# Gate and state stores of an mLSTM/GLA decoder step issued by SP behind the weight loads, in place of ScalarE

## What is computed

```python
a = rmsnorm(h, g_mix)
z = a @ w_in                      # 1024 x 8216: q, k, v and gates of both branches
hm, C, n, m = mlstm_scan(mq, mk, mv, li, lf, C0, n0, m0)
hg, Sf = gla_scan(gq, gk, gv, la, S0)
hm = head_layernorm(hm) * g_m * sigmoid(mo)
hg = head_rmsnorm(hg) * g_g * silu(gg)
h = h + (sigmoid(ga) * (hm @ w_pa) + sigmoid(gb) * (hg @ w_pb)) @ w_o
h = h + conv_ffn(rmsnorm(h), ...)           # w_up, depthwise conv, w_down
h = h + sigmoid(rmsnorm(h) @ w_ple_gate) * (p @ w_ple_proj)
y = rmsnorm(h, g_out)
```

## Time and profile before

| | |
|---|---|
| median of 3 runs | 1183.09 us |
| the profiled execution | 1183.06 us |
| its span, first to last instruction | 1181.2 us |
| TensorE busy | 1166.8 us (99%) |
| VectorE busy | 757.9 us (64%) |
| ScalarE busy | 393.1 us (33%) |
| first and last moved store issued | 115.3 us and 533.4 us |
| DMA on the SP queue, on ScalarE's queue | 89.39 MB, 47.77 MB |

### The profile page before, as it was taken

How to read it: one execution, slowest core, us unless ns; L and a number is a source line. 1 busy time by engine, 2 the same in 40 slices (tenths; PEclk the granted TensorE clock), 3 DMA queues, 4 the chain that set the end, 5 groups by cost and what they waited for, 6 DMA issues and landing times.

```text
span 1181.2 us, 21812 instructions
## 1 busy us (share of the span) xinstructions
PE 1166.8 (99%) x9169; PEld 1110.0 (94%) x9169; DVE 757.9 (64%) x1396; ACT 393.1 (33%) x576; POOL 2.3 (0%) x7
## 2 busy tenths in 40 slices
PE   9999999999999999999999999999999999999996
PEld 8999999999999999999999999999999999999995
DVE  6855568675777655664655667777777763333777
ACT  6243232134343322333343233333333322111544
POOL 0000000000000000000000000000000000000000
PEclk9999999999999999999999999999999999999998
DMA  6342232422312366563443542232222143223222
GB/s 220 112 145 90 90 108 90 144 72 93 113 67 109 133 228 212 177 199 120 153 155 114 172 147 72 72 108 72 75 105 72 61 163 107 72 94 98 77 99 81
DMA packets 48962, 138.56 MB, mean 117 GB/s; under 512 B 5460, under 2 KB 25108, under 8 KB 39776
## 3 DMA queue, kind: packets, MB, share of 16 engines
q1 hardware_dynamic: 16392, 89.39, 21.9%
q10 hardware_dynamic: 32472, 47.77, 12.0%
HBM read 113.15 MB, written 23.81 MB: 116 GB/s over the span
## 4 chain that ended last, share of the span: by engine, by line
PE 95%; issue 3%; DVE 1%; DMA 1%; ACT 1%; POOL 0%; ACTq 0%; POOLq 0%; DVEq 0%
PE ps L768 34%; PE ps L796 10%; PE ps L794 6%; PE ps L797 6%; PE ps L795 6%; PE ps L897 6%; PE ps L774 6%; PE ps L798 5%; PE ps L903 3%; PE ps L815 2%; PE aux L1060 1%; DMA xT<-in_xT 1%; PE aux L1124 1%; PE aux L955 1%; PE aux L1020 1%
## 5 line engine op out<-in xcount | busy, mean ns | idle before, releaser
L768 PE MATMUL ps<-apair,whi 128*128 128x288 f32 x1728 | 274.9, 298 | 0.6 <-ACT mq L2067 0.5
L768 PEld LDWEIGHTS ps<-apair,whi 128*128 128x128 f32 x1728 | 243.2, 188 | 4.9 <-issue 2.1
L1175 DVE TENSOR_TENSOR wlo<-wraw,whi 128x2048 fp32r<-128x2048 f32 (+1 forms) x82 | 176.1, 2147 | 74.8 <-ACT whi L1912 70.5
L1912 ACT ACTIVATE whi<-wraw 128x2048 fp32r<-128x2048 f32 (+1 forms) x87 | 156.4, 1797 | 106.2 <-PE ps L798 52.5
L796 PE MATMUL ps<-apair,whi 128*128 128x512 f32 x336 | 132.1, 393 | 0.0
L794 PE MATMUL ps<-apair,whi 128*128 128x320 f32 x336 | 105.0, 313 | 0.0
L797 PE MATMUL ps<-apair,wlo 128*128 128x320 f32 x336 | 104.2, 310 | 0.0
L795 PE MATMUL ps<-apair,whi 128*128 128x320 f32 x336 | 103.8, 309 | 0.0
L768 PE MATMUL ps<-apair,wlo 128*128 128x288 f32 x448 | 95.9, 296 | 0.0
L798 PE MATMUL ps<-apair,wlo 128*128 128x256 f32 x336 | 95.1, 283 | 0.0
L798 PEld LDWEIGHTS ps<-apair,wlo 128*128 128x128 f32 x336 | 63.2, 188 | 14.2
(11 more groups left out here) (405 smaller groups left out, 2091.5 us busy)
## 6 DMA issues: line engine op xcount, KB each, us to landing
wraw<-in_w_in SPq DMA_DIRECT2D x31, 1024.0 KB, 4.9
wraw<-in_w_up SPq DMA_DIRECT2D x21, 1024.0 KB, 4.8
gate_scratch<-stg ACTq DMA_DIRECT2D x32, 288.0 KB, 2.8
gt<-gate_scratch ACTq DMA_DIRECT2D x32, 288.0 KB, 2.9
wraw<-in_w_pgate SPq DMA_DIRECT2D x6, 1024.0 KB, 4.8
wraw<-in_w_down SPq DMA_DIRECT2D x8, 704.0 KB, 4.1
wraw<-in_w_down SPq DMA_DIRECT2D x8, 640.0 KB, 3.8
out_C_s<-st ACTq DMA_DIRECT2D x16, 256.0 KB, 2.8
```

What stands on the lines that cost most here:

```text
L768: mm = nc.tensor.matmul(ps[:, t % 2, a, 0:HALF], w, x(k)[:, a * HALF:(a + 1) * HALF], start=f, stop=e)
L1175: V.tensor_tensor(wlo[:, s, 0:n], wraw[:, s, 0:n], f32(whi[:, s, 0:n]), ALU.subtract)\
L1912: A.activation(whi[:, s, 0:n], wraw[:, s, 0:n], ACT.Copy).then_inc(split_hi, 1)
```

## The change

All 32 stores of gate tiles and all 32 stores of sample states (16 of C_s, 16 of S_s) are issued by SP. After SP has issued the load of unit u it goes through the entries of unit u - 3 in order, and for each gate tile and each hk waits for the eviction or the update and issues the store. ScalarE waits no longer for the evictions and updates before these stores, but for one `st_new` ahead of the store of n. Sizes, buffers, and what waits for the landings stay as they are.

```diff
+            def stores_of(u):
+                first, last = sched.index(("unit", u)), sched.index(("unit", u + 1))
+                for s in sched[first:last]:
+                    if s[0] == "tile" and units[s[1]][0] in ("mo", "gg", "ga", "gb"):
+                        t = tile_at[s]
+                        k = 2 * units[u][1] + s[2] + {"mo": ZMO, "gg": ZGG, "ga": ZGA, "gb": ZGB}[units[u][0]]
+                        sp.wait_ge(tile_free[t % 2], t // 2 + 1)
+                        sp.dma_start(zs[k, :, :], stg[:, k % 2, :]).then_inc(stg_out[k % 2], 16)
+                    elif s[0] == "hk":
+                        which, p, i = s[1:]
+                        sp.wait_ge(st_new, 4 * pair_no(which, p) + i + 1)
+                        dst = outs["C_s"] if which == "m" else outs["S_s"]
+                        for e in range(2):
+                            sp.dma_start(dst[2 * p + e, :, i:NB:4, :], st[e][:, i:NB:4, 0:DV]).then_inc(st_out[e][i], 16)
...
             for u, (kind, i) in enumerate(units):
...
+                if u >= 3:
+                    stores_of(u - 3)
...
-            late_out = [b for b, e in zip(sched, sched[1:]) if e[0] == "lev" and e[1] < NC and e[2] == 3]
-            after_levels = False
...
-                    elif kind in ("mo", "gg", "ga", "gb"):
-                        k = ng["stg"]
-                        ng["stg"] += 1
-                        after_levels = s in late_out
-                        if not after_levels:
-                            act.wait_ge(tile_free[tt % 2], tt // 2 + 1)
-                            act.dma_start(zs[k, :, :], stg[:, k % 2, :]).then_inc(stg_out[k % 2], 16)
...
                 elif s[0] == "hk":
                     which, p, i = s[1:]
                     q = pair_no(which, p)
-                    act.wait_ge(st_new, 4 * q + i + 1)
-                    dst = outs["C_s"] if which == "m" else outs["S_s"]
-                    for e in range(2):
-                        act.dma_start(dst[2 * p + e, :, i:NB:4, :], st[e][:, i:NB:4, 0:DV]).then_inc(st_out[e][i], 16)
+                    if which == "m" and p == 1 and i == 3:
+                        act.wait_ge(st_new, 4 * q + i + 1)
...
-                        if after_levels:
-                            k, after_levels = ng["stg"] - 1, False
-                            act.wait_ge(tile_free[tt % 2], tt // 2 + 1)
-                            act.dma_start(zs[k, :, :], stg[:, k % 2, :]).then_inc(stg_out[k % 2], 16)
```

## The result

The changed kernel took 1189.22 us in the median of 6 runs (1188.54 to 1190.99), against 1182.59 us for the kernel before (6 runs), a ratio of 1.0054 (95% interval 1.0043 to 1.0064): 6.6 us slower. The forecast was 1183.5 us, no change, in a range of 1182.4 to 1186.2. The change is clear of noise, and the time lies above the range.

What follows compares the result with a forecast made beforehand. The prediction took TensorE, busy 99% of the span, as the bound. To 1183.06 us it added 0 + 0 + 0 + 0.2 + 0.2 = +0.4 us, giving 1183.5 us, in a range of 1182.4 to 1186.2.

Steps and rivals of the forecast that it cites:

- What bounds the kernel: TensorE, busy 99% of the span, bounds the kernel; ScalarE's relief is real but gains nothing.
- Issue time: 30.4 us of store issuing moves from ScalarE's idle time to SP's waiting time: 0 gained, 0 lost.
- head of line on SP: Store waits of unit u - 3 ahead of the load of u + 1 on SP are always over first: 0.
- Landing after 5.8 us: The first tile's store, behind a 1 MB load, was estimated to land 5.8 us after the split's end.
- (b): ScalarE's reload of the last state piece waits for later store landings, ahead of bt m 0's sigmoid: +0.2 us.
- (c): VectorE waits for all state stores in bt m 4, beginning 2.0 to 2.7 us late, 1.98 covered: +0.2 us.
- (a): VectorE waits for a slot of `stg`, worst at 418.25 us, 1.7 to 2.5 us late with idle time behind: 0.
- the near range: At ScalarE's last reload, stores landing at 463.6 to 465.3 us, so -1.1 to +0.6 us.
- The slower one: Rival: ScalarE hangs at 463 us waiting for the last state stores, TensorE stands at 475 us: 1186.4 us, chance 0.17.
- The rule: Skill page on DMA: issuers share 16 engines, so by that rule alone the sum for the moved stores would be 0.

Runs made afterwards that it cites:

- experiments 1 and 2: The changed kernel with the first tile's and following hk's stores issued before the split wait and load (1182.43 us), then after the wait but before the load (1182.39 us).
- experiment 3: The changed kernel with all state stores back on ScalarE (first run, 1183.07 us), then with all gate stores back on ScalarE instead (second run, 1184.58 us).
- experiment 5: The changed kernel again, 1190.61 us; then with 14 idle products on TensorE ahead of the transposes of bt m 6 and bt m 7, 1186.68 us.
- Experiment 6: The changed kernel with all 64 stores issued by GpSimd in a queue of their own, at the same point, the load staying with SP: 1190.85 us.
- the second of experiment 4: The changed kernel with only the 8 state stores of pair g 0 back on ScalarE: 1186.52 us, ratio 1.0033.

## Why the prediction was wrong

- **What bounds the kernel**: right. Nothing was gained by ScalarE's relief; the kernels of experiments 1 and 2, which have it without the cost, take the time of before.
- **Issue time and head of line on SP**: right, both 0. No wait of TensorE is for a weight that landed late, and experiments 1 and 2 leave SP with the same issues.
- **Landing after 5.8 us**: too short. It was taken from the lone load (4.9 us) plus 0.9. Measured, the load takes 6.0 us in the median, and the first store behind it lands some 7 us after the load's issue (load issued at 304.74 and landed at 310.78, store landed at 312.06). The prediction had the row that told it: a store 1.5 us behind a load had landed after 6.2 us, and the load after 5.6. I used it to weigh a rule and not for the size.
- **The step that failed**: the sum took each landing by itself and held the two loads that (b) and (c) start from at the times of the trace before, "the load at 453.2 us" and "the load issued at 513.5". They were issued at 455.37 and 518.19. A store that lands late makes VectorE late, by itself or by ScalarE's reload, VectorE's split sets when SP issues the next load, and the next stores stand behind that load: a loop, which the sum had in (c) only as a bound ("if VectorE comes 1.8 us late through (a)").
- **(a), cost 0**: right for the gate stores alone, which cost 0.5 us, within noise. The estimate for 418.25 us was near (1.7 to 2.5 us late; it was 2.7, of which 0.2 are TensorE's lag), and it was absorbed. At 508 us it was too small: in the kernel with the gate stores alone (first run of experiment 3) the eviction begins at 510.83 in place of 508.53, 2.3 us late where "up to 1 us" stood, because the store ahead lands 7.1 us after the split's end and not 5.8. The next load is late by as much, 515.79 in place of 513.49.
- **(b), +0.2**: right mechanism, right place, and the slack of 0.1 us was right. ScalarE's table load came 2.8 us late (468.09 against 465.32), and TensorE's lag grew by 2.5. From the load's issue to the last landing the near range was right: it gives 10.4 to 12.1 us (453.2 to 463.6 and to 465.3), and 12.1 were measured (455.37 to 467.49). What was wrong is the start, 2.2 us late where the sum allowed 0.4: an earlier piece of the reload had waited for a state store, too.
- **(c), +0.2**: right mechanism, wrong size. bt m 4 began 7.7 us late, not 2.0 to 2.7. Of these, 2.8 us are TensorE's own lag from 475 us, 1.9 us the late load beyond that lag, and the other 3.0 the landing: the last store landed 8.3 us after that load's issue, where the sum had 7.4 to 8.1. Beyond the lag that is 5.0 us, and less the 1.98 us that the sum counted as covered it is 3.0; TensorE's lag grew by 3.1 there, against "0 to 0.7" and "up to 2.5" for the case that VectorE comes late, which is the one that came.
- **What was not in the sum**: the granted clock. A wait of TensorE was priced at its length. Here, behind two waits of 1.0 and 1.8 us, 1.5 us in one execution came on top, and 2.7 behind 1.4 and 1.8 us in another. The spread of the runs is 3.0 us over the 5 of the changed kernel in experiment 5 and 1.1 with the waits filled; that the clock makes it is likely, not shown.
- **The rivals.** The slower one had the place and the deciding point: the last hk 3 store landed at 467.49, past the 467.0 given. At 0.17 its chance was too low, and its price of 1186.4 left out that (a), (b) and (c) feed each other.
- **The rule.** The Trainium skill, "DMA: Bandwidth & Descriptors", section "Issuing engines are not separate DMA queues", says that issuers share the same 16 engines and a second one saves only sequencer time. Experiment 6 agrees: 6.3 us in another queue, 6.5 in the same. What I drew from the section "Queues, rings and completion order", that a store loses by sharing the load's queue, is not what the runs show. Two queues that are served in turn from the start would have let the store of experiment 6 in earlier; its first packet started 4.2 us after its issue, and it landed as late as in SP's queue. What costs is to be issued after the load at all.

## What to carry to other kernels

When a small store has someone waiting and a large load has not, issue the store first: here the swap of the two calls is worth 6.6 us, and the choice of the queue brings the store in no earlier. Before idle time is counted as cover for a later landing, ask whether the late engine sets when the next landing starts; if so it is a loop, and the start of the next transfer has to be worked out anew, not read from the trace before. A wait on a TensorE that was fully busy can cost more than its length: here 1.5 and 2.7 us more, by a fall of the granted clock.

## What was not expected of the hardware

- A store issued in another queue half a microsecond or more after a 1 MB load landed only after the load (6.3 us in the median), as one issued in the load's own queue did (6.5 us); the median with the first tiles' stores ahead was 2.3 us. There is one exception: a store issued at 410.99 landed 1.8 us before a load that took 9.7 us.
- The load itself suffers from stores right behind it: 6.0 us in the changed kernel and with GpSimd's queue, 5.4 with the stores ahead, 4.9 before.
- With a wait of 1.8 us ahead of bt m 7, and one of 0.2 to 1.4 us that ended 0.8 us before it, the granted clock was at its lower level for 3.4 us in three profiles (the changed kernel, the second of experiment 4, experiment 6) and for about 6.7 us in a fourth. Idle products in the waits kept it up. A single wait of 0.9 us at the same place (experiment 3), or of 0.6 to 1.4 us before the products with `wlo`, did not bring it down. Nor did a wait of 1.9 us from 6.2 us on in the changed kernel, so the length of the wait alone does not decide.
